# GDN on one core: ScalarE's cast ahead of a gate tile's silu, the state's update ahead of the addition to the outputs

## The chip, the cores and the metric

The kernel runs on one core of a Trainium2 chip. The metric is the device time in microseconds (us) of one execution. TensorE (PE) multiplies matrices into PSUM, VectorE (DVE), ScalarE (ACT) and GpSimd (POOL) work element by element, SyncE (SP) issues most transfers. The engines run their own instruction streams and wait for each other on semaphores.

## What is computed

One streaming step of a two-layer trunk: a feed-forward block, a mixer and a feed-forward block in each layer, each with a residual and a layer norm. The first mixer is a gated linear attention (GLA), the second a gated delta rule (GDN). There are 512 prompt tokens and 8 running streams of 16 tokens, so 640 tokens in all. For each value head the GDN part computes, chunk by chunk,

```python
v_new = u - einsum('bhid,bhdv->bhiv', w, s)
o = einsum('bhid,bhdv->bhiv', qc * exp(gcum), s) + einsum('bhij,bhjv->bhiv', att, v_new)
s = exp(g_last) * s + einsum('bhjd,bhjv->bhdv', k_end, v_new)
```

and then `(rms_norm(o, norm_g) * silu(z)) @ w_o`, where `z` is a projection of the input by its own weights.

## The kernel before

**Weights.** All weights stream in as chunks of 128 x 1024 float32 into two buffers, `raw` even and odd. ScalarE casts a chunk to its high part `wh` (`act_split`, L245), POOL subtracts to get the low part `wl` (`pool_supply`, L277), and TensorE multiplies a tile of 640 tokens as three products, high by high, high by low and low by high (L227 and L525). The cast of chunk T+2 overwrites the buffer of chunk T, so it waits for `tile_done` of T. A tile's result in PSUM (`gem`, two slots) is taken out before the slot is used again (`evacuated`). SyncE loads the next chunk into `raw` when POOL's subtraction of the old one is done.

**The GDN phase.** It goes through eight key heads of two value heads each. Each engine has its own `body(hf, i, last)`. Heads 0 to 3 are one hardware loop, heads 4 to 6 another, and head 7 is written out behind the second (`last`); after heads 3 and 7 a projection with the `hh` and `hl` tiles follows. TensorE weaves the weight tiles of the next head (four tiles) and of the head's own gate `z` (two tiles, numbers 4 and 5) between the small products of the head, in eighths of a tile (`parts`).

**The part around the change.** A head ends with a walk over four prompt steps t = 0 to 3 of 128 tokens. In step t TensorE multiplies keys and queries by the state `d_s` (L1186, L1187; from step 1 it waits for the state of step t-1), VectorE forms `d_w` (`less_old`, L1611), TensorE multiplies by the inverse (L1208), ScalarE scales this to the new values (`new_values`, L1395), and TensorE computes the step's outputs into `msc[:, 3]` (L1216) and the state's update into `msc[:, 0]` (L1220). VectorE then adds the outputs to `d_o` (`outputs`, L1618) and forms the new state (L1666). In steps 0 and 1 VectorE also has the convolution of the next head (`convolve(3, ...)`, L1435 to L1453). In steps 1 and 2 TensorE multiplies the running streams' states (L1195) into the other half of `msc[:, 3]`; in step 3 it transposes those results (L1202) into `msc[:, 3]` and `msc[:, 2]`.

Behind step 3 VectorE goes on with `key_ends` (L1603), the decay of the streams' states (L1624), `spread_values` (L1630) and the streams' outputs (L1618 once more). ScalarE squares the outputs (L1381) and takes a square root (L1415); VectorE normalizes (L1681) and adds the streams' new states (L1638, twice). For these (`on` and `s_new`) TensorE waits before it transposes the outputs (L1250). VectorE multiplies these with the gate (`gate_outputs`, L1644) and splits the product into `hh` and `hl` (`split_hidden`, L907 and L909), first for value head 0, then for 1. The next head's first transposes (L510) wait for the two gatings, a projection's last tiles for the splits.

Meanwhile ScalarE, after the square root, takes out the two gate tiles (`tile_out(4)`, `tile_out(5)`): it waits for the tile, applies the silu (L1331) and then casts the chunk that comes next into that buffer (`act_split`). Then it issues the stores of the states (L1419, L1420).

Of the kernel before, what the change touches and what calls it, by code (L numbers as in the profile page):

```python
# [106 lines left out]
def build(nc, wstream, x_in, consts, ln_cols, w_a1, w_a2, b_a, norm_cols, w_ab, a_dt, conv_w, hist_in,  # L107
          gla_s, gdn_s, y_out, gla_p_out, gdn_p_out, hist_out, gla_s_out, gdn_s_out):
    with ExitStack() as ctx:
# [70 lines left out]
        def half(T):  # L180
            return T // 2 if isinstance(T, int) else T.half
# [49 lines left out]
        def slot(par):  # L231
            return gem[:, par, :, 0:HALF]

        def halves(ap):
            return ap.rearrange("p (s n) -> p s n", s=2)

        def act_split(act, T, par):

            if isinstance(T, int) and T + 2 >= N_CHUNKS:
                return  # L240
            nxt = half(T) + 1
            act.wait_ge(loaded[par].sem, loaded[par].at(nxt))
            if not (isinstance(T, int) and T < 0):
                act.wait_ge(tile_done.sem, tile_done.at(T))
            act.copy(wh[:, par, :], raw[:, par, :]).then_inc(hi_ready.sem, hi_ready.by)  # L245
# [254 lines left out]
        def col(t, n=P):  # L500
            return slice(t * n, (t + 1) * n)
# [471 lines left out]
        def num(name, t, v):  # L973
            return d_hq[:, GN.index(name), t, v:v + 1]

        gdn = {n: Signal("gdn_" + n, per=p) for n, p in dict(
            ab_mm=1, gates=7, gact=5, cum_mm=1, cact=3, copied=1, zero=1, cum=1, neg=1, conv_h=1,
            hq=1, qk_mm=2, sq=NU, ss=1, std=1, rs=2, qt=1, kt=1, v_mm=2, v=2, kq_mm=2, kq=2, kk_mm=1, kk=2, qkm_mm=1,
            qkm=1, dt_mm=2, dt=2, att=2, m=2, ml=2, p_mm=12, p=12, y_mm=12, t=10, u=14, ex=2, cleared=2,
            s_zero=1, ks_mm=TT, f_mm=2, f=2, w=TT, a=TT, ke=TT, tw_mm=TT, vn=TT, o_mm=TT, o=TT, su_mm=PT, state=PT,  # L980
            vx=1, ssu_mm=1, s_dec=2, s_new=2, osq=NU, oss=1, ostd=1, ors=1, on=1, og_mm=2, og=2, split=2).items()}
# [19 lines left out]
        def gdn_tile(hf, i, n, last):  # L1001

            return tile(gdn_start(hf), 6, i, n - 4 if last else n)

        def unit(v, t):
            return TT * v + t
# [4 lines left out]
        def after(lv, v):  # L1011

            return 2 * lv + v
# [11 lines left out]
        def pe_gdn(pe, occ):  # L1025
# [33 lines left out]
            def body(hf, i, last=False):  # L1059
                s = i + 4 * hf  # L1060
# [117 lines left out]
                ks, qs, tw, o = (msc[:, j, 0:2 * P] for j in range(4))  # L1178
                for t in range(PT):
                    if t == 0:  # L1180
                        pe.wait_ge(gdn["s_zero"].sem, gdn["s_zero"].at(s))
                        pe.wait_ge(gdn["u"].sem, gdn["u"].at(s, after(LEVELS - 1, 1)))
                    else:
                        pe.wait_ge(gdn["state"].sem, gdn["state"].at(s, t - 1))
                    both = d_s.rearrange("p v n -> p (v n)")
                    pe.matmul(ks, d_kq[:, 0, col(t)], both, start=True, stop=True)  # L1186
                    pe.matmul(qs, d_kq[:, 1, col(t)], both, start=True, stop=True)\  # L1187
                      .then_inc(gdn["ks_mm"].sem, gdn["ks_mm"].by)
                    if t in (1, 2):
                        v = t - 1  # L1190
                        pe.wait_ge(d_sld.sem, d_sld.at(s))
                        out = msc[:, 3, 2 * P:4 * P].rearrange("p (a n) -> p a n", a=2)
                        for r in range(STREAMS):
                            c0 = r * SLEN
                            mm = pe.matmul(out[:, :, c0:c0 + SLEN], d_sin[:, v, r, :],  # L1195
                                           d_kq[:, :, SEQ + c0:SEQ + c0 + SLEN], start=True, stop=True)
                        mm.then_inc(gdn["f_mm"].sem, gdn["f_mm"].by)
                    if t == 3:
                        pe.wait_ge(gdn["f"].sem, gdn["f"].at(s, 1))
                        for j in range(2):  # L1200
                            for v in range(2):
                                mm = pe.transpose(msc[:, 3 - j, col(2 * j + v)], d_f[:, v, j, :], ident)  # L1202
                        mm.then_inc(gdn["ks_mm"].sem, gdn["ks_mm"].by)
                    a, b, c, d = SEQ_PARTS[t]
                    parts(a, b)
                    pe.wait_ge(gdn["w"].sem, gdn["w"].at(s, t))
                    for v in range(2):
                        mm = pe.matmul(tw[:, col(v)], d_U[:, unit(v, t), :], d_w[:, v, :], start=True, stop=True)  # L1208
                    mm.then_inc(gdn["tw_mm"].sem, gdn["tw_mm"].by)
                    parts(b, c)  # L1210
                    pe.wait_ge(gdn["vn"].sem, gdn["vn"].at(s, t))
                    pe.wait_ge(gdn["att"].sem, gdn["att"].at(s, 1))
                    if t == PT - 1:
                        pe.wait_ge(gdn["w"].sem, gdn["w"].at(s, PT))
                    for v in range(2):
                        mm = pe.matmul(o[:, col(v)], d_at[:, unit(v, t), :], d_vn[:, v, :], start=True, stop=True)  # L1216
                    mm.then_inc(gdn["o_mm"].sem, gdn["o_mm"].by)
                    pe.wait_ge(gdn["ke"].sem, gdn["ke"].at(s, t))
                    for v in range(2):
                        mm = pe.matmul(ks[:, col(v)], d_ke[:, v, :], d_vn[:, v, :], start=True, stop=True)  # L1220
                    mm.then_inc(gdn["su_mm"].sem, gdn["su_mm"].by)
                    parts(c, d)
# [43 lines left out]
        def act_gdn(act, occ):  # L1266
# [46 lines left out]
            def body(hf, i, last=False):  # L1313
                s = i + 4 * hf
# [7 lines left out]
                def tile_out(j):  # L1322

                    T = gdn_tile(hf, i, j, last)
                    if j < 4:
                        if not last:
                            conv_in(T, j % 2, s * 4 + (4 + j), False)
                        return
                    act.wait_ge(tile_done.sem, tile_done.at(T))
                    act.wait_ge(gdn["att"].sem, gdn["att"].at(s, 1))  # L1330
                    act.activation(halves(d_z[j - 4]), slot(j % 2), ACT.Silu).then_inc(evacuated[j % 2].sem, evacuated[j % 2].by)  # L1331
                    act_split(act, T, j % 2)
                for j in range(2):
                    act.wait_ge(gdn["qk_mm"].sem, gdn["qk_mm"].at(s, j))
                    for t in range(TT):
# [89 lines left out]
        def dve_gdn(dve, occ):  # L1425
# [72 lines left out]
            def body(hf, i, last=False):  # L1498
                s = i + 4 * hf
# [98 lines left out]
                def key_ends(t):  # L1598
                    dve.wait_ge(gdn["kt"].sem, gdn["kt"].at(s))
                    if t:  # L1600
                        dve.wait_ge(gdn["su_mm"].sem, gdn["su_mm"].at(s, t - 1))
                    for v in range(2):
                        ins = dve.tensor_scalar(d_ke[:, v, :], d_kt[:, t, :], num("ke", t, v), None, ALU.mult)  # L1603
                    ins.then_inc(gdn["ke"].sem, gdn["ke"].by)
# [10 lines left out]
                def outputs(t):  # L1615
                    dve.wait_ge(gdn["o_mm"].sem, gdn["o_mm"].at(s, t))
                    dve.wait_ge(gdn["a"].sem, gdn["a"].at(s, t))
                    dve.tensor_tensor(d_o[:, t], d_o[:, t],  # L1618
                                      msc[:, 3, 0:2 * P].rearrange("p (v n) -> p v n", v=2), ALU.add)\
                       .then_inc(gdn["o"].sem, gdn["o"].by)  # L1620
# [27 lines left out]
                for t in range(PT):  # L1648
                    key_ends(t)
                    less_old(t)  # L1650
                    if t == 0:
                        convolve(3, range(0, 2))
                    if t == 1:
                        convolve(3, range(2, CONV))
                    if t == 2:
                        decay_stream(0)
                    if t == 3:
                        less_old(PT)
                    outputs(t)
                    dve.wait_ge(gdn["su_mm"].sem, gdn["su_mm"].at(s, t))  # L1660
                    if t == 0:
                        dve.wait_ge(gdn["s_zero"].sem, gdn["s_zero"].at(s))
                    else:
                        dve.wait_ge(gdn["state"].sem, gdn["state"].at(s, t - 1))
                    for v in range(2):
                        ins = dve.scalar_tensor_tensor(out=d_s[:, v, :], in0=d_s[:, v, :],  # L1666
                                                       scalar=num("egl", t, v), in1=msc[:, 0, col(v)],
                                                       op0=ALU.mult, op1=ALU.add)
                    ins.then_inc(gdn["state"].sem, gdn["state"].by)
                key_ends(PT)  # L1670
                decay_stream(1)
                dve.wait_ge(gdn["vn"].sem, gdn["vn"].at(s, PT))
# [196 lines left out]
```

## Time and profile before

| | |
|---|---|
| three runs | 3332.34 us median, 3322.84 to 3341.79 |
| the profiled execution | 3329.35 us, its span 3326.7 us |
| TensorE's mean granted clock in it | 0.952 of full speed |
| TensorE matmuls busy | 3144.0 us, 95% of the span |
| VectorE, ScalarE, POOL busy | 1352.5, 1020.3 and 1002.7 us |
| GDN phase | from about 1885 to 2765 us of the span |

The span is from the first to the last instruction. The busy share is an average over stages with different limits, so the questions for a stage are who waits for whom there and whose wait ends last. In the trace's answers a row with `[x <-E L]` had x us of idle time on its engine ahead of it, which ended with work of engine E at line L; a row without brackets had none. `xN` says that N instructions stand in one row. The ends of matmuls are modelled.

### The profile page before, as it was taken

What the parts mean: (1) busy time and instruction counts of PE and PEld (TensorE: products, weight loads), DVE (VectorE), ACT (ScalarE), POOL (GpSimd) and SP (SyncE); (2) the same over time, 40 slices, a digit from 0 to 9 for tenths busy, and PEclk for the clock granted to TensorE, in tenths of its full rate; (3) what the DMA queues carried; (4) which work ended last, traced back from release to release, by engine and by line L of the source; (5) the groups of instructions that cost most, each with busy time, mean ns of one, the idle gap of its engine ahead of it and who ended that gap; (6) DMA issues with size and microseconds to landing.
All of it is one profiled execution on the core that took longest, in us unless ns stands there. A gap on an engine that the chain in (4) does not pass through costs nothing.

```text
span 3326.7 us, 63652 instructions
## 1 busy us (share of the span) xinstructions
PE 3144.0 (95%) x25820; PEld 3008.1 (90%) x25820; DVE 1352.5 (41%) x1913; ACT 1020.3 (31%) x1766; POOL 1002.7 (30%) x412
## 2 busy tenths in 40 slices
PE   8999989998899999899999889989989979999997
PEld 8999987887899999899999878888988868999997
DVE  3222261224521213621314566666366656322126
ACT  2111135223331112431112444443344432421112
POOL 3333342221433333433333311111211103433332
PEclk9999998998899999899999889999998979999998
DMA  3122221111122222122222111111111112122222
GB/s 129 70 76 82 76 70 51 68 69 72 51 76 76 76 82 76 57 76 76 76 82 76 41 50 54 60 60 60 64 61 60 40 41 78 63 71 75 82 76 75
DMA packets 61233, 228.95 MB, mean 69 GB/s; under 512 B 7185, under 2 KB 9233, under 8 KB 57762
## 3 DMA queue, kind: packets, MB, share of 16 engines
q1 hardware_dynamic: 55906, 200.04, 17.0%
q10 hardware_dynamic: 5184, 26.74, 2.2%
q8 instruction: 122, 2.00, 0.2%
q14 instruction: 21, 0.17, 0.0%
HBM read 209.53 MB, written 17.22 MB: 68 GB/s over the span
## 4 chain that ended last, share of the span: by engine, by line
PE 70%; issue 21%; POOL 4%; DVE 3%; ACT 2%; POOLq 0%; DVEq 0%; ACTq 0%
PE gem L227 57%; PE gem L525 6%; POOL wl L277 2%; POOL xl L475 1%; PE msc L417 1%; PE msc L669 1%; PE msc L688 1%; PE msc L677 1%; DVE work L386 0%; PE msc L410 0%; PE msc L510 0%; DVE hh L907 0%; PE msc L611 0%; PE msc L1115 0%; PE msc L1124 0%
## 5 line engine op out<-in xcount | busy, mean ns | idle before, releaser
L277 POOL TENSOR_TENSOR wl<-raw,wh 128x1024 fp32r<-128x1024 f32 x368 | 939.6, 2553 | 2224.7 <-ACT wh L245 2224.7
L245 ACT CAST wh<-raw 128x1024 fp32r<-128x1024 f32 x368 | 386.8, 1051 | 1422.8 <-PE gem L227 1402.2
L227 PE MATMUL gem<-xh,wh 128*128 128x320 f32 x2688 | 612.9, 309 | 4.7 <-POOL wl L277 4.7
L227 PE MATMUL gem<-xh,wl 128*128 128x320 f32 x2688 | 612.6, 309 | 0.0
L227 PE MATMUL gem<-xl,wh 128*128 128x320 f32 x2688 | 612.2, 309 | 0.0
L227 PEld LDWEIGHTS gem<-xh,wh 128*128 128x128 f32 x2688 | 449.4, 188 | 5.7 <-POOL wl L277 5.7
L227 PEld LDWEIGHTS gem<-xl,wh 128*128 128x128 f32 x2688 | 449.5, 188 | 0.0
L227 PEld LDWEIGHTS gem<-xh,wl 128*128 128x128 f32 x2688 | 449.2, 188 | 0.0
L344 DVE TENSOR_TENSOR work<-work,gem 128x640 f32<-128x640 f32 x88 | 72.3, 821 | 879.3 <-PE gem L227 843.3
L227 PE MATMUL gem<-hh,wh 128*128 128x320 f32 x1792 | 409.5, 310 | 1.6 <-DVE hl L909 1.6
L227 PE MATMUL gem<-hl,wh 128*128 128x320 f32 x1792 | 408.8, 309 | 0.0
L227 PE MATMUL gem<-hh,wl 128*128 128x320 f32 x1792 | 408.6, 309 | 0.0
L525 PE MATMUL gem<-xh,wh 128*128 128x320 f32 x1280 | 340.3, 349 | 40.7 <-POOL wl L277 15.7
L525 PE MATMUL gem<-xl,wh 128*128 128x320 f32 x1280 | 310.8, 326 | 6.9 <-POOL xl L475 6.9
L525 PE MATMUL gem<-xh,wl 128*128 128x320 f32 x1280 | 309.9, 325 | 0.0
L227 PEld LDWEIGHTS gem<-hh,wh 128*128 128x128 f32 x1792 | 299.9, 188 | 2.6 <-DVE hl L909 2.1
L227 PEld LDWEIGHTS gem<-hl,wh 128*128 128x128 f32 x1792 | 300.2, 188 | 0.0
L227 PEld LDWEIGHTS gem<-hh,wl 128*128 128x128 f32 x1792 | 300.1, 188 | 0.0
L372 DVE SCALAR_TENSOR_TENSOR x<-x,gem 128x640 f32 (+1 forms) x120 | 98.6, 822 | 481.1 <-PE gem L227 481.1
L525 PEld LDWEIGHTS gem<-xh,wh 128*128 128x128 f32 x1280 | 222.4, 203 | 69.6 <-issue 39.3
L349 DVE TENSOR_TENSOR hl<-work,hh 128x640 f32 (+1 forms) x88 | 242.5, 2756 | 10.7
L525 PEld LDWEIGHTS gem<-xl,wh 128*128 128x128 f32 x1280 | 231.4, 203 | 8.8 <-POOL xl L475 8.8
(256 smaller groups left out, 3000.0 us busy)
## 6 DMA issues: line engine op xcount, KB each, us to landing
raw<-wstream SPq DMA_DIRECT2D x368, 512.0 KB, 3.2
work<-gdn_s ACTq DMA_DIRECT2D x8, 1024.0 KB, 4.8
gdn_s_out<-work ACTq DMA_DIRECT2D x8, 1024.0 KB, 4.3
work<-gla_s ACTq DMA_DIRECT2D x4, 1024.0 KB, 5.3
gla_s_out<-work ACTq DMA_DIRECT2D x4, 1024.0 KB, 3.9
x<-x_in SPq DMA_DIRECT2D x2, 1280.0 KB, 7.9
y_out<-x SPq DMA_DIRECT2D x8, 320.0 KB, 2.2
gdn_p_out<-work ACTq DMA_DIRECT2D x8, 128.0 KB, 5.4
```

What stands on the lines that cost most here:

```text
L227: mm = pe.matmul(gem[:, par, s, 0:HALF], w, r[:, k, s * HALF:(s + 1) * HALF], start=(k == 0 and n == 0), stop=(k == kts - 1 and n == 2))
L245: act.copy(wh[:, par, :], raw[:, par, :]).then_inc(hi_ready.sem, hi_ready.by)
L277: pool.tensor_tensor(wl[:, par, :], raw[:, par, :], wh[:, par, :].bitcast(F32), ALU.subtract)\
L344: dve.tensor_tensor(halves(hid), halves(gate), slot(1), ALU.mult)\
L349: dve.tensor_tensor(hl[:, i, :], hid, hh[:, i, :].bitcast(F32), ALU.subtract)\
L372: dve.scalar_tensor_tensor(out=halves(xt), in0=halves(xt), scalar=scale, in1=slot(par), op0=ALU.mult, op1=ALU.add).then_inc(evacuated[par] ...
L417: mm = pe.matmul(msc[:, b + s, 0:HALF], ones, flat[:, s * HALF:(s + 1) * HALF], start=True, stop=True)
L475: pool.tensor_tensor(xl[:, k, :], x[:, k, :], xh[:, k, :].bitcast(F32), ALU.subtract)\
L525: mm = pe.matmul(gem[:, par, s, 0:HALF], w, r[:, k, s * HALF:(s + 1) * HALF], start=(k == 0 and n == 0), stop=(k == KT - 1 and n == 2))
L669: pe.matmul(msc[:, 2 + c, 0:2 * P], a_ket[rows, t, :], a_vt[rows, t, :], start=True, stop=True)\
L677: pe.matmul(msc[rows, t % 2, 0:2 * P], a_qd[:, n * GLA_CHUNK:(n + 1) * GLA_CHUNK], a_s, start=False, stop=True, skip_group_check=True)\
L688: mm = pe.matmul(msc[:, 2, d * P + s * SLEN:d * P + (s + 1) * SLEN], a_sin[:, s, d, :], a_qd[:, c0:c0 + SLEN], start=True, stop=True)
```

## The change

In `act_gdn`, `tile_out` for the gate tiles issues the cast of the next chunk ahead of the silu instead of behind it. In `dve_gdn` the call `outputs(t)` moves behind the state's update in the four prompt steps. Because TensorE, which waits for the state, can no longer conclude from it that the outputs of that step are read, `pe_gdn` gets a wait for them ahead of the products into the same banks: in steps 1 and 2 ahead of L1195, in step 3 ahead of L1202.

```diff
                     if t in (1, 2):
                         v = t - 1
                         pe.wait_ge(d_sld.sem, d_sld.at(s))
+                        pe.wait_ge(gdn["o"].sem, gdn["o"].at(s, t - 1))
                         out = msc[:, 3, 2 * P:4 * P].rearrange("p (a n) -> p a n", a=2)
...
                     if t == 3:
                         pe.wait_ge(gdn["f"].sem, gdn["f"].at(s, 1))
+                        pe.wait_ge(gdn["o"].sem, gdn["o"].at(s, t - 1))
                         for j in range(2):
...
                     act.wait_ge(gdn["att"].sem, gdn["att"].at(s, 1))
+                    act_split(act, T, j % 2)
                     act.activation(halves(d_z[j - 4]), slot(j % 2), ACT.Silu).then_inc(evacuated[j % 2].sem, evacuated[j % 2].by)
-                    act_split(act, T, j % 2)
...
                     if t == 3:
                         less_old(PT)
-                    outputs(t)
                     dve.wait_ge(gdn["su_mm"].sem, gdn["su_mm"].at(s, t))
...
                     ins.then_inc(gdn["state"].sem, gdn["state"].by)
+                    outputs(t)
                 key_ends(PT)
```

## Rows read from the trace of the kernel before

**Rows 1.** Page, part 1: engines, busy us, share of the span, instructions

```profile
PE 3144.0 (95%) x25820; PEld 3008.1 (90%) x25820; DVE 1352.5 (41%) x1913; ACT 1020.3 (31%) x1766; POOL 1002.7 (30%) x412
```

**Rows 2.** Waits of TensorE, 1885 to 2765 us: total us, times, longest

```profile
PE gem L525 <- POOL wl L277: 13.4, 4, 3.6
...
PE msc L1186 <- DVE work L1666: 7.4, 7, 1.3
...
PE msc L510 <- DVE work L1644: 4.2, 2, 3.6
...
PE gem L227 <- DVE hl L909: 1.6, 2, 1.0
```

**Rows 3.** Timeline, TensorE, second head: start, us, instruction, idle before

```profile
2097.51 0.70 PE L1186 MATMUL msc<-work 128*128 128x256 f32 x2 [1.28 <-DVE work L1666]
...
2102.13 0.61 PE L1220 MATMUL msc<-work 128*128 128x128 f32 x4
...
2123.54 1.28 PE L1250 MATMUL msc<-cs,work 128*128 128x128 f32 x10
2128.41 0.55 PE L525 MATMUL gem<-xh,wh 128*128 128x320 f32 x2 [3.59 <-POOL wl L277]
```

**Rows 4.** Timeline, VectorE, second head

```profile
2096.52 0.42 DVE L1618 TENSOR_TENSOR work<-work,msc 128x256 f32<-128x256 f32 x1
2096.85 0.60 DVE L1666 SCALAR_TENSOR_TENSOR work<-work,gq,msc 128x128 f32<-128x128 f32 x2
...
2098.68 0.61 DVE L1611 SCALAR_TENSOR_TENSOR work<-msc,gq,work 128x128 f32<-128x128 f32 x2 [0.83 <-PE msc L1187]
...
2102.34 0.42 DVE L1618 TENSOR_TENSOR work<-work,msc 128x256 f32<-128x256 f32 x1 [1.01 <-PE msc L1216]
2102.78 0.60 DVE L1666 SCALAR_TENSOR_TENSOR work<-work,gq,msc 128x128 f32<-128x128 f32 x2
...
2119.64 1.49 DVE L1681 TENSOR_TENSOR work<-work,gq 128x1280 f32<-128x1280 f32 x1
2121.05 2.35 DVE L1638 TENSOR_TENSOR work<-work,msc 128x1024 f32<-128x1024 f32 x2
```

**Rows 5.** Timeline, ScalarE, end of the second head

```profile
2119.15 0.21 ACT L1415 ACTIVATE gq<-gq 128x10 f32<-128x10 f32 x1
2119.38 1.28 ACT L1331 ACT_TABLE_LOAD   x1
...
2121.27 1.04 ACT L245 CAST wh<-raw 128x1024 fp32r<-128x1024 f32 x1
2123.55 0.71 ACT L1331 ACTIVATE work<-gem 128x640 f32<-128x640 f32 x1 [1.24 <-PE gem L525]
```

**Rows 6.** Timeline, POOL, end of the second head

```profile
2122.39 2.39 POOL L277 TENSOR_TENSOR wl<-raw,wh 128x1024 fp32r<-128x1024 f32 x1 [27.21 <-ACT wh L245]
2125.26 2.34 POOL L277 TENSOR_TENSOR wl<-raw,wh 128x1024 fp32r<-128x1024 f32 x1 [0.48 <-ACT wh L245]
```

**Rows 7.** Timeline, TensorE, from head 3 to the projection

```profile
2318.90 0.56 PE L227 MATMUL gem<-hh,wh 128*128 128x320 f32 x2
...
2325.48 0.56 PE L227 MATMUL gem<-hh,wh 128*128 128x320 f32 x2 [1.04 <-DVE hl L909]
```

**Rows 8.** Timeline, VectorE, second head: under and beside a subtraction of POOL

```profile
2041.33 0.91 DVE L1446 SCALAR_TENSOR_TENSOR work<-work,convw 128x664 f32<-128x664 f32 x1 [0.16 <-DVE work L1443]
...
2125.43 2.52 DVE L907 CAST hh<-work 128x640 f32 x1
```

**Rows 9.** Timeline, POOL, in the same place as the first of rows 8

```profile
2041.46 3.02 POOL L277 TENSOR_TENSOR wl<-raw,wh 128x1024 fp32r<-128x1024 f32 x1 [11.74 <-ACT wh L245]
```

**Rows 10.** One line's instructions, L1638: ns min/median/max, first and last start

```profile
L1638 DVE TENSOR_TENSOR work<-work,msc x16: 1215/1216/1218, 2023.2 to 2752.5; 128x1024 f32<-128x1024 f32 x16
```

**Rows 11.** Windows, two heads from L1250 to L1250: us, busy, granted clock

```profile
2123.54:2220.03 96.49, 85.75 (x1248) 78.08 (x1249) 64.57 (x140) 44.11 (x124) 14.88 (x7) 0.98 0.16 58
...
2565.41:2665.81 100.40, 92.65 (x1249) 84.46 (x1249) 64.03 (x140) 44.11 (x124) 14.89 (x7) 0.90 0.16 55
```

## Prediction

> **What bounds the kernel now.** I read the engines' shares first: TensorE's matmuls are busy 95% of the span [rows 1], so an edit on ScalarE or VectorE counts only where TensorE waits for it. The change touches the GDN phase alone (eight heads, about 880 of 3327 us), so next I read who TensorE waited for in that stretch [rows 2]. Four rows matter: L525 for POOL's `wl` (13.4 us, 4 times), L1186 for the state's update (7.4 us, 7 times), L510 for the gating L1644 (4.2 us, twice), L227 for `hl` (1.6 us, twice). Even all of it would be 26.6 us, 0.8% of the time. Then I followed the second head instruction by instruction [rows 3 to 6]. The other heads show the same pattern, except that the last has no convolution and its L1186 does not wait.
>
> **Part 1: the state's update ahead of the addition.** At step 0 VectorE comes late out of a convolution, so the addition (L1618 at 2096.52) and the update (L1666 at 2096.85) run back to back, 0.33 us apart. TensorE, whose update product is long done, waits 1.28 us and starts L1186 at 2097.51, 0.06 us after the update's end [rows 3, 4]. Reordered, the update starts 0.33 us earlier and so does L1186, in the seven heads that wait there. At step 1 the two instructions stand 0.44 us apart (2102.34 and 2102.78), not 0.33: the update waits for the product L1220, which ends at 2102.13 + 0.61 = 2102.74 [rows 3, 4]. The addition only fills that wait. Reordering gains nothing there, and steps 2 and 3 have the same distance (0.45). But the addition now comes after the update: 0.33 us more before `key_ends`. After steps 0 to 2 VectorE idles 0.83 us for the next L1187 before L1611 [rows 4], which hides it. After step 3 nothing hides it: `key_ends`, the decay, `spread_values`, the last addition, the squares, the normalization L1681 and the two L1638 follow in one chain.
>
> Who is late at the head's end? The second L1638 ends at 2121.05 + 2.35 = 2123.40 and the transposes L1250 start at 2123.54 [rows 3, 4]. This lag is 0.14 to 0.15 us in all eight heads, also in the last, where TensorE's own work reaches that point differently. So VectorE's chain already sets L1250, not TensorE. In heads 0 to 6 that chain gets 0.33 us at step 0 and pays 0.33 us behind step 3: **zero**, and TensorE's gain becomes a wait of the same size before L1250. Head 7, which gains nothing at step 0, pays **+0.33 us** at its L1250.
>
> The three added waits of TensorE per head (outputs of step t-1) are met: the addition of step 0 would end near 2097.5, and the instruction behind the wait, L1195, comes after L1186 and L1187, past 2098. Queued behind each is TensorE's whole stream, and behind that VectorE's `less_old`. A wait that is already met has no row of its own. From below it costs nothing, since TensorE's queue runs ahead of the array; less than nothing is excluded, a wait starts no matmul earlier. From above: L1250, behind two waits, starts 0.14 us after its releaser, L1186 behind one 0.06 us [rows 3, 4], so 0.08 us each. 24 waits give 0 to 1.9 us. I take **+0.5 us**, nearer to nothing, because these are met some 0.6 us ahead.
>
> **Part 2: the cast ahead of the silu.** After the square root (2119.15) ScalarE loads a table (1.28 us), does the first z tile's silu (0.71) and casts the next chunk at 2121.27 [rows 5]; POOL's first subtraction starts at 2122.39 [rows 6]. The chunk and the z tile are long there, so the cast moves to about 2119.38 and ends by 2120.42, if it needs no table of its own: a cast after a square root elsewhere in the head loads none. POOL could start at 2120.50, inside L1681 (2119.64 to 2121.13 [rows 4]), which reads two SBUF operands. Rows show what happens then: L1446 starts first (2041.33) and keeps its 0.91 us, and the subtraction started at 2041.46 takes 3.02 us [rows 8, 9] where 2.34 to 2.39 is usual [rows 6]. So it ends near 2123.5 in place of 2124.78: 1.3 us earlier. L1638, with an operand in PSUM, takes 1215 to 1218 ns in all its 16 places [rows 10], the second of each pair under POOL's subtraction, so it does not suffer. The silu slips by a cast, about 1.05 us, to 2122.4; its reader L1644 comes after 2124.4: hidden.
>
> The second z tile: today its silu starts at 2123.55 with the end of TensorE's tile, and the cast follows 0.60 us later. Cast first, and the tile itself 0.33 us earlier by part 1, give 0.92 us: POOL's second subtraction runs 2124.34 to 2126.7 instead of 2125.26 to 2127.60 [rows 5, 6]. That one matters: the cast L907 takes 2.52 us [rows 8] as it stands behind it. So the second gating L1644 and the `hl` split come 0.9 us earlier.
>
> Where does TensorE wait for these? From head 6 to head 7, L510 waits 3.6 us, its longest, for the second gating [rows 2]: **-0.9 us**. From head 3 to the projection L227 waits 1.04 us for `hl` [rows 7]: **-0.9 us**. At the last projection the wait is the other 0.5 of the 1.6 us [rows 2] and the chain starts 0.33 us later, so the gain shrinks to **-0.5 us** with that 0.33 still to be paid. At the other five seams, where the loop jumps back, TensorE restarts before or with that chain; one of them may give 0.2 us, which I leave out.
>
> At those five seams lies the largest gap: L525 starts 3.59 us after L1250's end, and the view names POOL [rows 3]. But POOL's subtraction of this very chunk had ended at 2124.78, 3.6 us before. From head 3 to the projection, where no loop jumps back, L227 follows L1250 without idle time at 2318.90 [rows 7], though its chunk was as late. The gap is 2.48 to 3.59 us at all five jumps and absent at the other three seams. So I hold it for the jump, and the earlier cast does not shorten it.
>
> The Trainium skill, page "Runtime: NRT & Kernel Launch", section "Instruction fetch mechanics", says that a taken branch out of the fetched window must fetch its target by DMA first. By that rule the gap stays; by the view's label the earlier chunk would shorten it by 1.3 us five times, which is the first rival.
>
> **Sum.** +0.3 + 0.5 - 0.9 - 0.9 - 0.5 = **-1.5 us**. Against the profiled execution (3329.35 us with 3326.7 us of span) that is 3327.9. That execution lies 3.0 us under the median of the runs, 3332.34, so for a median I take **3330.8 us**.
>
> **The rivals.**
> *The seam waits for POOL after all.* For it: the label [rows 2, 3]. Against it: 3.6 us between POOL's end and the restart. Price: five times 1.3 us more, -8 in all: 3324.3.
> *Slower: POOL takes the port from L1681.* If the subtraction started ahead of L1681, that would stand behind it as L907 does, by up to 2.39 us, and L1250 with it, since VectorE's chain sets it: eight times, +19: 3350. It decides from the point where the cast ends before 2119.64, 0.8 us sooner than I reckon; a start inside L1681 would do it only if a running instruction could be held up, which L1446 speaks against.
> The Trainium skill, page "SBUF — State Buffer", section "SBUF: two separate sides", calls the pair an exclusive lock that goes to whoever starts first; by it L1681 keeps its time.
> *The clock.* Heads take 96.49 us at a granted clock of 0.98 and 100.40 at 0.90 [rows 11]. The drops to half speed come in stretches of some us after sparse work, and moved waits can move them. Five looped heads by half that spread: 10 us either way, 3321 to 3341.
> *The cast does not come earlier*, because the table load goes ahead of it: then only part 1 is left, +0.8: 3333.
>
> **How the numbers follow.** Forecast 0.68, seam 0.10, clock 0.12, collision 0.05, table 0.05. A measurement of this kernel tells about 0.5%, 16.7 us, from no change. All cases but the collision lie inside; outside I put what the runs' own scatter (3322.84 to 3341.79), a clock case beyond its bound and a seam that closes altogether (five times 3.2, 3316) can bring: faster 0.09, slower 0.07, same 0.84. The range takes the forecast with its wait bounds (-2.0 to +1.4 about it), the clock's 10 us and the seam: 3317 to 3343.
>
> **What would show it.** L1186 of step 1 should wait about 0.95 us in the second head and L1250 should start 0.14 us after L1638 as before. The addition after step 3 should stand behind the update. POOL's first subtraction at a head's end should last about 3.0 us, its start under L1681, and L510's wait in head 7 should fall to about 2.7 us, L227's to nearly none. Wrong would be: seams near 2 us, L1681 longer than 1.49 us, or TensorE idle at L1195 or L1202.

## The result, and the profile after

| | before | after |
|---|---|---|
| median of 20 runs each, us | 3333.3 (3322.84 to 3344.37) | 3345.56 (3331.36 to 3352.92) |
| ratio to before | | 1.0034, interval 1.0023 to 1.0044 |
| profiled execution, its span, us | 3329.35, 3326.7 | 3335.88, 3334.1 |
| TensorE's mean granted clock in it | 0.952 | 0.954 |
| five gaps of TensorE at the loop jumps, sum, us | 15.93 | 23.93 |

The change costs about 12 us, and the interval does not reach 1. By the bound of 0.5% this counts as no change, the outcome given 0.84, but the time lies 2.6 us above the range, and the sign of the forecast difference (-1.5 us) was wrong. The profiled execution of after is the second fastest of its 20, 9.7 us under their median, so its span understates the loss. A gap is counted here from the end of the transposes (their start plus 1.28 us) to the start of TensorE's next matmul. The line numbers of after are two higher from L1197 on (the transposes L1250 are L1252, L1638 is L1640, L1644 is L1646, L1666 is L1667, L1681 is L1683, and the silu's L1331 is L1334).

TensorE's waits in the GDN phase of after, 1885 to 2775 us: total us, times, longest. They answer [rows 2].

```profile
PE gem L525 <- issue: 26.7, 9, 5.4
PE msc L1124 <- issue: 14.7, 13, 2.2
...
PE msc L1186 <- DVE work L1667: 5.3, 6, 0.9
...
PE msc L510 <- DVE work L1646: 3.3, 2, 2.8
...
PE msc L1252 <- DVE work L1640: 2.8, 8, 0.4
...
PE gem L227 <- DVE hl L909: 0.7, 2, 0.5
```

Every wait that the change was to shorten is shorter: L1186 7.4 to 5.3 us, L510 4.2 to 3.3, L227 1.6 to 0.7. L1252, which had no row before, now waits 0.36 to 0.37 us in seven heads and 0.29 us in the last. The first row is the loss. Before, L525 had 13.4 us under POOL [rows 2] and, in the same view,

```profile
PE msc L1124 <- issue: 11.0, 10, 1.7
...
PE gem L525 <- issue: 4.9, 5, 2.5
```

Now all of it stands under "issue", and it is 8.4 us more. L1124 also grew, by 3.7 us, but it does not go with the time: it is 13.7 us in e5, whose time is before's within its interval, and 17.0 in e10, which is faster (both below).

The second head of after on TensorE, VectorE and POOL: start, us, instruction, idle before in brackets, with ScalarE's cast and table load. They answer [rows 3 to 6].

```profile
2099.95 0.70 PE L1186 MATMUL msc<-work 128*128 128x256 f32 x2 [0.92 <-DVE work L1667]
...
2123.52 1.03 ACT L245 CAST wh<-raw 128x1024 fp32r<-128x1024 f32 x1
2124.57 1.28 ACT L1334 ACT_TABLE_LOAD   x1
...
2123.90 1.49 DVE L1683 TENSOR_TENSOR work<-work,gq 128x1280 f32<-128x1280 f32 x1
2125.30 2.35 DVE L1640 TENSOR_TENSOR work<-work,msc 128x1024 f32<-128x1024 f32 x2
...
2124.63 3.02 POOL L277 TENSOR_TENSOR wl<-raw,wh 128x1024 fp32r<-128x1024 f32 x1 [27.08 <-ACT wh L245]
2128.68 2.35 POOL L277 TENSOR_TENSOR wl<-raw,wh 128x1024 fp32r<-128x1024 f32 x1 [1.02 <-ACT wh L245]
...
2127.80 1.28 PE L1252 MATMUL msc<-cs,work 128*128 128x128 f32 x10 [0.36 <-DVE work L1640]
2133.78 0.90 PE L525 MATMUL gem<-xh,wh 128*128 128x320 f32 x2 [4.70 <-issue]
```

L1186 waits 0.92 us, not 1.28; POOL's first subtraction starts under L1683, lasts 3.02 us, and L1683 keeps its 1.49. Up to the transposes the head went as reckoned. Then comes the jump, and the gap is 4.70 us in place of 3.59 [rows 3]. At the five jumps the gaps were 2.49, 3.59, 3.32, 3.35 and 3.18 us before; after, 4.48, 4.70, 4.24, 5.06 and 5.45. At the three seams without a jump they are 0 to 0.5 us in both.

What fills the gap shows in the transfer queues. Rows of quarter-us windows in the second head (queue: packets, MB, share of 16 engines; a packet's whole time is booked where it starts, so a share can pass 100%), first of before, 2125.79 to 2126.04 us, that is 2.25 us after L1250 starts:

```profile
q10 hardware_dynamic: 14, 0.11, 113.4%
q8 instruction: 1, 0.02, 23.6%
```

and of after, 2131.05 to 2131.30 us, 3.25 us after L1252 starts:

```profile
q10 hardware_dynamic: 5, 0.04, 49.1%
q8 instruction: 1, 0.02, 22.0%
q1 hardware_dynamic: 4, 0.02, 15.9%
```

q8 carries instructions: one packet of 16 KB. It stands in this place at every one of the five jumps, and at none of the three other seams. q10 is the store of the streams' states (`gdn_s_out`, 1024 KB, issued by ScalarE), q1 SyncE's load into `raw`. I take q8's packet for the fetch of TensorE's instructions, since TensorE restarts about 2.6 us after it here (before: 3.59 + 1.28 - 2.25 = 2.6; after: 4.70 + 1.28 - 3.25 = 2.7). The traces bear this out: at each of the 60 jumps in the twelve profiles exactly one q8 packet starts between the transposes and the restart, and TensorE restarts 1.4 to 1.9 us after that packet's end. So the packet came 1 us later, with the store's packets running ahead of it. The issues of these transfers, before and then after:

```profile
2123.69 0.34 ACTq L1419 DMA_DIRECT2D gdn_s_out<-work  x1
2124.96 3.15 SPq L270 DMA_DIRECT2D raw<-wstream  x2
```

```profile
2127.68 0.34 ACTq L1421 DMA_DIRECT2D gdn_s_out<-work  x1
2127.83 3.70 SPq L270 DMA_DIRECT2D raw<-wstream  x2
```

Counted from the transposes (2123.54 and 2127.80), the store went from 0.15 us behind to 0.12 ahead (0.115 before rounding, so -0.11 below), the load from 1.42 behind to 0.03 behind. Both parts of the change moved a transfer toward the fetch. Part 1: TensorE's last weight tile ends 0.33 us earlier against VectorE's chain (that is the 0.36 us wait at L1252), so ScalarE is past that tile when the new states are ready, and its store goes out at once. Part 2: POOL frees `raw` earlier (2127.65 in after, 0.15 us ahead of the transposes; 2124.78 in before, 1.24 us behind), so SyncE loads earlier.

### The profile page after: what moved, and what is told of

Same layout as the page of the kernel before. It is cut to its first block, busy times and chain, and to the rows that moved or that the text cites. A ratio compares the mean times of both kernels' runs of the same rounds, so it can differ in the third digit from the quotient of the medians.

```text
span 3334.1 us, 63676 instructions
## 1 busy us (share of the span) xinstructions
PE 3138.2 (94%) x25820; PEld 3001.5 (90%) x25820; DVE 1344.1 (40%) x1913; ACT 1019.3 (31%) x1766; POOL 1007.6 (30%) x412
## 4 chain that ended last, share of the span: by engine, by line
PE 70%; issue 21%; POOL 4%; DVE 4%; ACT 2%; POOLq 0%; DVEq 0%; ACTq 0%
PE gem L227 57%; PE gem L525 6%; POOL wl L277 2%; POOL xl L475 1%; PE msc L417 1%; PE msc L669 1%; PE msc L688 1%; PE msc L677 1%; PE msc L410 0%; DVE work L386 0%; PE msc L510 0%; DVE hh L907 0%; PE msc L1124 0%; PE msc L611 0%; ACT x L430 0%
## 5 line engine op out<-in xcount | busy, mean ns | idle before, releaser
L227 PE MATMUL gem<-xh,wh 128*128 128x320 f32 x2688 | 612.8, 309 | 4.7 <-POOL wl L277 4.7
L227 PE MATMUL gem<-xl,wh 128*128 128x320 f32 x2688 | 612.6, 309 | 0.0
L227 PE MATMUL gem<-xh,wl 128*128 128x320 f32 x2688 | 612.3, 309 | 0.0
L227 PEld LDWEIGHTS gem<-xh,wh 128*128 128x128 f32 x2688 | 449.1, 188 | 5.7 <-POOL wl L277 5.7
L227 PEld LDWEIGHTS gem<-xh,wl 128*128 128x128 f32 x2688 | 449.5, 188 | 0.0
L227 PEld LDWEIGHTS gem<-xl,wh 128*128 128x128 f32 x2688 | 449.3, 188 | 0.0
L227 PE MATMUL gem<-hh,wh 128*128 128x320 f32 x1792 | 409.5, 310 | 0.7 <-DVE hl L909 0.7
L227 PE MATMUL gem<-hl,wh 128*128 128x320 f32 x1792 | 408.9, 309 | 0.0
L227 PE MATMUL gem<-hh,wl 128*128 128x320 f32 x1792 | 408.6, 309 | 0.0
L525 PE MATMUL gem<-xh,wh 128*128 128x320 f32 x1280 | 338.0, 347 | 49.0 <-issue 26.7
L525 PE MATMUL gem<-xl,wh 128*128 128x320 f32 x1280 | 308.9, 324 | 7.2 <-POOL xl L475 7.2
L525 PE MATMUL gem<-xh,wl 128*128 128x320 f32 x1280 | 308.1, 324 | 0.0
L227 PEld LDWEIGHTS gem<-hh,wh 128*128 128x128 f32 x1792 | 299.9, 188 | 1.2 <-DVE hl L909 1.2
L227 PEld LDWEIGHTS gem<-hh,wl 128*128 128x128 f32 x1792 | 300.2, 188 | 0.0
L227 PEld LDWEIGHTS gem<-hl,wh 128*128 128x128 f32 x1792 | 300.2, 188 | 0.0
L525 PEld LDWEIGHTS gem<-xh,wh 128*128 128x128 f32 x1280 | 220.6, 202 | 77.9 <-issue 62.4
L525 PEld LDWEIGHTS gem<-xl,wh 128*128 128x128 f32 x1280 | 229.6, 202 | 9.2 <-POOL xl L475 9.2
```

The source lines that it names most:

```text
L227: mm = pe.matmul(gem[:, par, s, 0:HALF], w, r[:, k, s * HALF:(s + 1) * HALF], start=(k == 0 and n == 0), stop=(k == kts - 1 and n == 2))
L525: mm = pe.matmul(gem[:, par, s, 0:HALF], w, r[:, k, s * HALF:(s + 1) * HALF], start=(k == 0 and n == 0), stop=(k == KT - 1 and n == 2))
```

## The experiments

All gaps are the sums of the five jumps in each kernel's own profile, which is one execution. Offsets are from the start of the transposes; a packet's is the start of the quarter us in which it lies. Ratios are to the kernel before on the same chip, medians of 12 runs (reorder: 7).

| run | gaps, us | store issued | load issued | fetch's packet | ratio (interval) |
|---|---|---|---|---|---|
| before | 15.93 | +0.15 | +1.42 | 1.0 to 2.25 | 1 |
| after | 23.93 | -0.11 | +0.03 | 2.75 to 4.0 | 1.0034 (1.0023 to 1.0044) |
| e1 first cast | 20.23 | +0.16 | +0.04 | 1.0 to 3.75 | 1.0024 (1.001 to 1.0038) |
| e2 second cast | 15.45 | +0.20 | +1.41 | 1.0 to 1.5 | 0.9989 (0.9977 to 1.0001) |
| e3 reorder | 23.12 | -0.11 | +1.40 | 2.75 to 3.75 | 1.0036 (1.0021 to 1.0052) |
| e4 after, store later | 18.19 | +4.3 to 5.0 | +0.03 | 1.0 to 2.5 | 1.0013 (0.9998 to 1.0028) |
| e5 waits alone | 15.89 | +0.15 | +1.42 | 1.0 to 2.0 | 1.0004 (0.9991 to 1.0018) |
| e6 before, store earlier | 21.78 | -0.11 | +1.41 | 2.5 to 3.5 | 1.0025 (1.0008 to 1.0042) |
| e7 reorder, store later | 14.17 | +3.6 to 4.0 | +1.40 | 1.0 to 1.5 | 0.9988 (0.9974 to 1.0002) |
| e8 second cast, store later | 14.44 | +3.6 to 4.3 | +1.41 | 1.0 to 1.75 | 0.9977 (0.9963 to 0.9991) |
| e9 after, store and load later | 14.35 | +3.6 to 4.1 | +3.7 to 4.2 | 1.0 to 1.5 | 0.9983 (0.9972 to 0.9994) |
| e10 reorder, second cast, store later | 13.79 | +3.6 to 4.1 | +1.41 | 1.0 | 0.9984 (0.9971 to 0.9996) |

**The parts one by one.** The kernel before with the cast ahead of the silu for tile 4 alone (e1), or for tile 5 alone (e2), and the reorder with its waits, casts as before (e3, the diff of `pe_gdn` and `dve_gdn` shown ahead). The first theory, S, was that part 2's earlier load into `raw` is what holds up the fetch; its rival, R, that the reorder with its waits costs the time by itself.

```diff
-                    act_split(act, T, j % 2)
+                    if j not in (4,):
+                        act_split(act, T, j % 2)
```

(and the cast `if j in (4,)` ahead of the silu; 5 for e2)

> The kernel before with the cast ahead of the silu for the first gate tile alone (tile 4); nothing else. Theory S (the earlier first subtraction lets SyncE load raw some 1.4 us earlier; that load runs beside the state's store when TensorE jumps back and fetches its instructions): the five gaps at the jumps, 2.48 to 3.59 us before (15.9 in all), become 4.2 to 5.5 us (about 24), raw's load is issued within 0.2 us of L1250's start, and the time is 8 to 12 us above before. Theory R (the moved addition and TensorE's three added waits cost the time): gaps as before, time within 2 us of before. Theory C (only the granted clock moved): gaps as before, time anywhere within 10 us.

> The kernel before with the cast ahead of the silu for the second gate tile alone (tile 5). Theory S: the first subtraction ends where it did, so the gaps stay at 15.9 us in all (within 1.5), and the second subtraction 0.6 us earlier takes 0.6 us off L510's wait in head 7 and off L227's wait behind head 3 and 0.5 behind head 7: 1.5 to 2 us below before. Theory R: the same, for it the cast is harmless. If any earlier subtraction lengthens the gaps, they grow here too, by less than in the other run.

> The reorder alone: the state's update ahead of the addition, with TensorE's three waits; the casts as before. Theory S: the gaps stay at 15.9 us in all (within 1.5); L1186 of step 1 waits 0.33 us less in seven heads and L1250 waits as much more; time between 1 us below and 2 us above before. Theory R: the time rises by 8 to 12 us, and TensorE is idle in front of L1195, L1202 or at the jumps.

Measured: the first cast alone costs 7 to 8 us (3340.67 to 3333.47 beside it, and the ratio), with gaps of 20.2 us where some 24 were expected. The second cast alone gains 4.9 us at the median, but its interval just reaches 1; its load stands as in before, its store 0.05 us later. The reorder alone costs 8.0 us and has nearly all of after's gaps, 23.12 us, though its load comes at +1.40 as in before. So S fell, by which the reorder was to change nothing. R had the time right, but it goes into the gaps, not into TensorE's waits. What the reorder has in common with after is the store at -0.11. The second head of e3 on TensorE, and the quarter us (2129.60 to 2129.85) in which its fetch comes:

```profile
2126.60 1.28 PE L1252 MATMUL msc<-cs,work 128*128 128x128 f32 x10 [0.36 <-DVE work L1640]
2132.26 0.89 PE L525 MATMUL gem<-xh,wh 128*128 128x320 f32 x2 [4.38 <-issue]
```

```profile
q10 hardware_dynamic: 9, 0.07, 84.0%
q8 instruction: 1, 0.02, 23.7%
```

Only the store's queue runs beside the fetch here. The two effects don't add: 23.1 with the store, 20.2 with the load, 23.9 with both. The second theory, T, was therefore that whatever starts ahead of the fetch holds it up.

**Is it the store, or the longer program?** The reorder has three more instructions in TensorE's loop body. Its rival, L, was that these shift the jump or its target in the instruction memory. e5 has the three waits and nothing else. e6 leaves TensorE's program as it was and issues the stores ahead of the last `tile_out`. e4 is after with the stores held until TensorE has entered its next body or projection.

The edit of e6:

```diff
                 tile_out(4)
-                tile_out(5)
                 act.wait_ge(gdn["s_new"].sem, gdn["s_new"].at(s, 1))
...
+                tile_out(5)
```

and of e4 (the late stores of e7 to e10 are the same lines):

```diff
                 s = i + 4 * hf
+                pe.sem_inc(passed.sem, passed.by)
...
                 gdn_loop(pe, hf, body)
+                pe.sem_inc(passed.sem, passed.by)
...
                 act.wait_ge(gdn["s_new"].sem, gdn["s_new"].at(s, 1))
+                act.wait_ge(passed.sem, passed.at(s, 1 + hf))
```

> The changed kernel, with the two stores of the states (gdn_s_out, gdn_p_out) issued only when TensorE has entered the next body or the projection (one counter that TensorE raises at the top of each, on which ScalarE waits ahead of the stores). Theory S: nothing but raw's load is left beside the instruction fetch, the gaps fall to 2.5 us or less each (under 13 in all, against 23.9), and the time falls by at least 10 us against the changed kernel, to before or below it. Theory R: the gaps do not depend on the stores and stay at 4.2 to 5.5 us, time as the changed kernel, 12 us above before.

> The kernel before with TensorE's three added waits alone; VectorE and ScalarE as before. Theory T (the traffic that starts ahead of the instruction fetch delays it: in the reorder the state's store is issued 0.11 us ahead of L1250 instead of 0.15 behind it): the waits move no transfer, so the store stays at +0.15, the five gaps at about 15.9 us in all (within 1.5), the time within 2 us of before. Theory L (three more instructions in TensorE's loop body shift the jump or its target in instruction memory): the gaps become 4.3 to 5.2 us, 23 in all, and the time rises by 6 to 9 us.

> The kernel before with ScalarE's two stores of the states issued ahead of the second gate tile (tile 5) instead of behind it; TensorE's and VectorE's programs are untouched. Theory T: the store is issued at about -0.1 us from L1250 and the gaps become 20 to 24 us in all, the time 4 to 8 us above before, without the reorder. Theory L: TensorE's instructions are the same as before, so the gaps stay at 15.9 and the time within 1 us.

Measured: with the waits alone the gaps are 15.89 us, before's, and the time is the same within its interval, so L is excluded and the waits themselves cost nothing that shows. With the store 0.26 us earlier, and TensorE's program, POOL's first subtraction and the load where they were, they are 21.78 us and the kernel is 8.3 us slower. The second head of e6, with the quarter us of its fetch (2133.04 to 2133.29):

```profile
2129.13 2.39 POOL L277 TENSOR_TENSOR wl<-raw,wh 128x1024 fp32r<-128x1024 f32 x1 [27.22 <-ACT wh L245]
2132.90 2.92 POOL L277 TENSOR_TENSOR wl<-raw,wh 128x1024 fp32r<-128x1024 f32 x1 [1.37 <-ACT wh L245]
...
2130.29 1.28 PE L1250 MATMUL msc<-cs,work 128*128 128x128 f32 x10
2135.83 0.83 PE L525 MATMUL gem<-xh,wh 128*128 128x320 f32 x2 [4.26 <-POOL wl L277]
```

```profile
q10 hardware_dynamic: 7, 0.06, 57.5%
q8 instruction: 1, 0.02, 22.0%
```

The view names POOL again for a gap that an earlier store lengthened; POOL's first subtraction ends 1.23 us behind the transposes' start (1.24 in before). One thing did move with the store: ScalarE reaches tile 5 only after it, so the second subtraction starts 0.89 us later than in before (2.61 us behind the transposes' start, not 1.72). In the head shown it ends at 2135.82, 0.01 us ahead of the restart, but that is chance: at two of the other four jumps TensorE restarts 0.2 us before it ends, at two 0.7 and 1.35 us after, always 2.6 to 2.7 us after the start of the fetch's packet. e4 took 5.7 us of gaps from after, but left 18.19 us where under 13 was expected, and some 7 us of time by the ratios where at least 10 was: the load at +0.03 still lies ahead of the fetch.

**Both out of the way.** e7 is e3, e8 is e2, and e10 both together, each with the late stores. e9 is e4 with SyncE's load at the five jumps held until TensorE is past the jump (SyncE's loop over the GDN chunks written out, `passed` among the waits of five of them).

What e9 has beside e4's lines:

```diff
+            def load(T, par, seam=None):
+                sp.wait_ge(lo_ready.sem, lo_ready.at(T) - 2)
+                if seam:
+                    sp.wait_ge(passed.sem, seam)
...
+                seams[first + 6 * (s - 4 * hf) + 8] = s + 2 + hf
```

> The reorder alone with its three waits, and the stores issued only when TensorE has entered the next body or the projection. Theory T: neither the store nor raw's load (issued 1.4 us behind L1250) starts ahead of the fetch, so the gaps fall below those of before, to 2.5 us or less, under 12.5 in all; the time comes to 2 to 5 us below before, and so the reorder by itself costs less than 1 us. Theory L: gaps stay above 4 us, time 6 to 9 us above before.

> The kernel before with the cast ahead of the silu for tile 5 alone and the stores issued only when TensorE has entered the next body or the projection. Theory T: gaps under 12.5 us in all, against 15.5 with that cast alone; with its 2 us the time comes to 5 to 8 us below before, the fastest so far. Theory L: gaps as with the cast alone or longer by the counter's instruction, time within 3 us of before.

> The whole changed kernel, with both transfers moved behind the jump: the two stores wait for TensorE's entry into the next body or projection, and at the five jumps SyncE's load of the even raw buffer waits for the same counter (SyncE's loop over the chunks is written out for the GDN phase for this). Theory T: the gaps fall from 18.2 us (stores moved alone) to 13 to 15 us in all, and the time to 4 to 8 us below before, 15 us or more below the changed kernel; so both parts of the change, freed of the collision, gain what they were reckoned to (about 2 us). If the parts cost something of their own, the gaps fall likewise and the time stays within 2 us of before.

> The reorder with its waits, the cast ahead for tile 5 alone, the stores behind the jump; the first subtraction and raw's load stay where they were. Theory T: gaps 14 to 14.5 us in all as in the two kernels it joins, time 5 to 8 us below before. The reorder should add nothing to the kernel with the second cast and the later stores (6.3 us below before): within 2 us of it.

Measured: the reorder with a late store has 14.17 us of gaps in place of 23.12 and 3328.7 us in place of 3341.47. After with both transfers late has 14.35 in place of 23.93, and lies 4.8 us under the kernel before beside it. The fetch now starts with nothing beside it; the quarter us of the second head's fetch in e7 (2118.11 to 2118.36), with its restart, and the restart of e9, whose L540 and L1268 are L525 and L1252:

```profile
q8 instruction: 1, 0.02, 30.1%
...
2121.32 0.81 PE L525 MATMUL gem<-xh,wh 128*128 128x320 f32 x2 [2.93 <-POOL wl L277]
```

```profile
2122.38 1.29 PE L1268 MATMUL msc<-cs,work 128*128 128x128 f32 x10 [0.37 <-DVE work L1658]
2126.77 0.56 PE L540 MATMUL gem<-xh,wh 128*128 128x320 f32 x2 [3.11 <-issue]
```

The gaps did not fall under 12.5 us in e7 and e8, as had been expected. A jump with nothing in its way still costs 2.6 to 3.3 us, and the most that before had to gain was some 2 us of gaps. e8 has the lowest ratio, 0.9977, and beats both kernels: 3326.65 us against 3332.96 beside it. e9 and e10 have intervals that overlap e8's, so which of these is best isn't settled. The reorder adds nothing that shows to e8 (e10).

**What a us of gap costs.** Over the eleven kernels the ratio follows the sum of the gaps (correlation 0.97), at 1.85 us of time for each us of gap. Each sum is of one execution. Part of the excess goes with the mean granted clock that each run lists: averaged over a kernel's runs it is 0.949 to 0.950 in after, e1, e3, e4 and e6, 0.951 to 0.954 in the others and in before. A line through all 223 runs with both terms gives 0.95 us for each us of gap and 1.8 us for each 0.001 of clock. For after that makes 8.0 x 0.95 = 7.6 us for the gaps and some 4 us for the clock, of 12.3. Why the clock is lower with longer gaps is shown only in part. TensorE in three windows (span, PE busy with matmul count, PE loads, DVE, ACT, POOL, then the granted clock, DMA share, GB/s): the gap of before's second head and the 10 us after its restart, and 10 us after the same restart in e2, whose gap was 2.70 us:

```profile
2124.82:2128.41 3.59, 0.01 (x1) 0.01 (x1) 3.33 (x3) 0.36 (x1) 2.34 (x1) 1.00 0.98 338
2128.41:2138.41 10.00, 10.00 (x60) 9.96 (x61) 4.73 (x11) 5.18 (x22) 0.00 (x0) 0.83 0.25 93
```

```profile
2132.14:2142.14 10.00, 9.83 (x69) 9.26 (x70) 5.54 (x13) 6.34 (x26) 0.00 (x0) 1.00 0.34 120
```

A clock of 0.83 is a mixture of the two levels (2.4 and 1.2 GHz); in it 60 matmuls were done, at full clock 69. Of the 60 jumps in the twelve profiles 11 were followed by 10 us at 1.00; their gaps were 2.59 to 3.06 us, and 14 others of 2.49 to 3.04 us were followed by less. So a shorter gap may save clock as well. But both before and after show a lower clock behind all five jumps, so this does not explain their difference in mean clock, and the single profile of after happens to be at 0.954. That the 4 us come from the gaps is argued, not shown.

## Why the prediction was wrong

**Part 1, the steps.** Right: L1186 of step 1 waits 0.92 us (0.95 predicted), and the saving is given back: L1252 waits 0.36 us, which the text had as "a wait of the same size before L1250". L1252 starts 0.15 us behind L1640, as before. The three waits have no cost that shows: e5 lies 1.9 us over before, with an interval across 1, against +0.5 (0 to 1.9). Head 7, from transposes to transposes, grew from 88.09 to 88.76 us, where -0.9 at L510, +0.33 and some waits were reckoned; but 88.09 is the shortest of all twelve kernels (the experiments have 88.45 to 90.02), so single executions do not settle terms of this size.

**Part 2, the steps.** Nearly right: L510's wait in head 7 fell from 3.6 to 2.8 us (2.7 predicted), and L227's from head 3 to the projection from 1.04 to 0.46 [rows 7]. There "nearly none" was reckoned. POOL's second subtraction starts 0.88 us behind the transposes, not 1.72: 0.84 earlier (0.92 predicted). Together TensorE's waits at L510 and L227 fell by 0.9 and 0.9 us, 1.8 in place of 2.3. The cast did come ahead of the table load, and the collision with L1681 did not happen: POOL started 0.73 us after L1683 and took 3.02 us, L1683 its 1.49. That is what the Trainium skill has in "SBUF — State Buffer", section "SBUF: two separate sides", and the trace agrees. The rivals of the collision and of the table load are out.

**The step that failed** is the one on the seams: "So I hold it for the jump, and the earlier cast does not shorten it." The first half was right, and against the label. The second asked only whether the gap could get shorter. The argument treated the jump as having a price of its own, while its five values, 2.49 to 3.59 us in one kernel, already said that something else takes part. The jump's fetch is a transfer, and it competes with the transfers that start ahead of it. The Trainium skill's rule on taken branches ("Runtime: NRT & Kernel Launch", section "Instruction fetch mechanics") holds here, by q8's packet at each of the five jumps. I put a constant in place of that fetch. The gap measured 2.6 to 3.3 us with nothing in the way (e7, e8, e10), and 4.2 to 5.5 us in after.

The step before it failed with it: of a moved cast the text followed POOL, L907 and TensorE, and not that POOL's end releases SyncE's load of 512 KB (1.4 us earlier, e1: +7 to 8 us), and of the reorder not that TensorE's earlier tile releases ScalarE's store of 1024 KB (0.26 us earlier, e3: +8.0 us, e6: +8.3 us with nothing else). The sum needed a term of +8.0 us, the gaps' own growth in the profile, in place of none. With the profile's 8.0 and the -1.5 us of the other terms the span would grow by 6.5 us; it grew by 7.4.

**The clock** was a rival of 10 us either way, worked out from the scatter between heads. Some 4 us of the loss go with a lower mean clock, but together with the gaps, and not as a case of its own. The range took the clock's 10 us above the forecast, and nothing for the seams above it: every case with seams was a faster one. Its lower wait bound, -2.0, is counted from before; about the forecast it is -0.5 (waits at nothing in place of 0.5). The time passed the upper end, which this does not touch.

**What would be wrong**, by the text: seams near 2 us, a longer L1681, or TensorE idle at L1195 or L1202. None came. Seams longer than before were not on the list, and they were the result.

## What to carry to other kernels

A hardware loop's jump can be a transfer of its own: look for the instruction queue's packet at each jump, and see which data transfers an edit moves ahead of it. Follow a moved step to the transfers that it releases, on whatever engine issues them; a store that goes out 0.26 us sooner cost this kernel 8 us. If a large store need not leave before the jump, hold it until the engine is in its next body: that was worth 5.7 to 9 us of gaps where the fetch had been behind it.

## What the runs showed of the hardware that was not expected

A single packet of 16 KB in the instruction queue came 1.0 to 1.75 us after the transposes' start with no data transfer ahead (e7 to e10), and 2.5 to 4.0 us when a 1024 KB store had been issued 0.11 us ahead of them (e3, e6, after). It did so although the data were in other queues. The whole step lies within 0.26 us of the store's issue: in before the store's first packets appear in the quarters from 0.75 or 1.0 us and the fetch in those from 1.0 to 2.25; in after they appear in the quarter from 0.5 and the fetch comes behind. The bytes moved during the gap are no measure of it: in the second head 338 GB/s in before's gap, 339 in after's, both at a DMA share of 0.97 to 0.98; in e10's gap of 3.04 us it is 0.44:

```profile
2129.08:2133.78 4.70, 0.00 (x1) 0.00 (x1) 4.27 (x5) 0.12 (x1) 1.95 (x1) 0.94 0.97 339
```

```profile
2120.67:2123.71 3.04, 0.01 (x2) 0.01 (x1) 2.78 (x3) 0.13 (x1) 2.26 (x1) 1.00 0.44 168
```

The first row is after's gap, the second e10's. Where in the path the packet waits, in a ring shared with the data or at the memory, no run here shows. Nor was it tried whether a smaller store ahead of the jump would cost less.
